# Routing by rounds of the eight largest, five buffers of expert weights, and the residual inside the sums

## The reference

```python
def expert_choice_ffn(h, w_router, w_gate, w_up, w_down):   # h: [1, 256, 1024]
    cap = EC_CAPACITY * S // N_EXPERTS                       # 32 tokens an expert, 16 experts
    aff = jax.nn.softmax(jnp.einsum('bsd,de->bse', h, w_router).astype(jnp.float32), axis=-1)
    g, idx = lax.top_k(aff.transpose(0, 2, 1), cap)          # each expert chooses its 32 tokens
    xe = h[bidx, idx]
    hid = (jax.nn.silu(jnp.einsum('becd,edf->becf', xe, w_gate))   # [1024, 2048] an expert
           * jnp.einsum('becd,edf->becf', xe, w_up))
    ye = jnp.einsum('becf,efd->becd', hid, w_down) * g[..., None].astype(h.dtype)
    return jnp.zeros_like(h).at[bidx, idx].add(ye)
# second_block ends with:
    x = x + expert_choice_ffn(h2, w_router[l], w_gate_e[l], w_up_e[l], w_down_e[l])
    return rms_norm(x, norm_f_g)
```

## Time and profile before

| | us |
|---|---|
| median of three runs | 1643.85 |
| profiled execution | 1641.73 |
| its span | 1639.9 |
| PE busy in the span | 1145.7 (70%) |
| DVE busy | 450.7 (27%) |
| ACT busy | 340.4 (21%) |
| chain that ended last: DMA | 51% |
| chain that ended last: PE | 35% |

### The profile page before, as it was taken

The page is one execution under the profiler, slowest core; times in us unless marked ns, Lnnn a source line. Parts: engine busy times, 40 slices in busy tenths (PEclk is TensorE's granted clock), DMA queues, the critical chain, the costliest instruction groups (busy, mean ns, idle before and its releaser), DMA issues.

```text
span 1639.9 us, 17750 instructions
## 1 busy us (share of the span) xinstructions
PE 1145.7 (70%) x7368; PEld 637.8 (39%) x7372; DVE 450.7 (27%) x742; ACT 340.4 (21%) x548; POOL 153.2 (9%) x119
## 2 busy tenths in 40 slices
PE   3997799996999867575656656566565556565654
PEld 1964798985998867331111111111111111111111
DVE  2457555555696764710000000000000000000001
ACT  3335444443445453100000000000000000000001
POOL 0110000003775300200000000000000000000000
PEclk8999899998999978787777877876888887778787
DMA  9877456553454311569999999999999999999996
GB/s 365 267 298 253 127 173 186 182 196 102 137 155 129 103 52 66 242 285 430 428 429 429 428 428 428 428 428 428 429 428 428 428 429 428 428 428 428 428 428 270
DMA packets 100410, 516.09 MB, mean 315 GB/s; under 512 B 7839, under 2 KB 64650, under 8 KB 72714
## 3 DMA queue, kind: packets, MB, share of 16 engines
q1 hardware_dynamic: 95328, 508.58, 77.2%
q10 hardware_dynamic: 4106, 4.63, 0.9%
q0 software_dynamic: 928, 2.20, 0.5%
HBM read 514.19 MB, written 1.07 MB: 314 GB/s over the span
## 4 chain that ended last, share of the span: by engine, by line
DMA 51%; PE 35%; DVE 9%; ACT 2%; issue 1%; POOL 0%; ACTq 0%; SPq 0%; POOLq 0%; DVEq 0%
DMA ring<-in_w_down_e 26%; DMA ring<-in_w_up_e 24%; PE PS L459 8%; PE PS L460 8%; PE PS L461 8%; PE PS L826 3%; PE PS L843 3%; DVE arena L1102 2%; PE PS L453 2%; DMA ring<-in_w_ada 1%; PE PS L514 1%; DVE arena L1098 1%; PE PS L805 1%; ACT hT L1425 1%; PE PS L593 1%
## 5 line engine op out<-in xcount | busy, mean ns | idle before, releaser
L826 PE MATMUL PS<-ring,arena 128*32 128x512 f32 x2048 | 332.2, 782 | 229.2 <-DMA ring<-in_w_up_e 122.8
L826 PEld LDWEIGHTS PS<-ring,arena 128*32 128x32 f32 x2048 | 63.6, 127 | 490.9 <-DMA ring<-in_w_up_e 207.7
L843 PE MATMUL PS<-ring,arena 128*32 128x512 f32 x1024 | 177.2, 827 | 107.8 <-DMA ring<-in_w_down_e 100.8
L1351 DVE TENSOR_TENSOR arena<-arena,PS 128x512 f32<-128x512 f32 x16 | 11.0, 688 | 865.1 <-PE PS L826 865.1
L459 PE MATMUL PS<-hR,wR 128*128 128x256 f32 x680 | 198.8, 292 | 25.3 <-DVE wR L352 16.0
L344 ACT ACTIVATE wR<-ring 128x1024 fp32r<-128x1024 f32 (+2 forms) x150 | 150.3, 1051 | 226.2 <-PE PS L461 226.1
L460 PE MATMUL PS<-hR,wR 128*128 128x256 f32 x680 | 196.8, 289 | 0.0
L461 PE MATMUL PS<-hR,wR 128*128 128x256 f32 x680 | 196.5, 289 | 0.0
L352 DVE TENSOR_TENSOR wR<-ring,wR 128x1024 fp32r<-128x1024 f32 x106 | 124.9, 1222 | 104.9 <-ACT wR L344 104.9
L459 PEld LDWEIGHTS PS<-hR,wR 128*128 128x128 f32 x680 | 135.2, 199 | 28.0 <-issue 22.4
L460 PEld LDWEIGHTS PS<-hR,wR 128*128 128x128 f32 x680 | 135.2, 199 | 0.1
(11 more groups left out here) (248 smaller groups left out, 1171.1 us busy)
## 6 DMA issues: line engine op xcount, KB each, us to landing
ring<-in_w_gate_e SPq DMA_DIRECT2D x64, 2048.0 KB, 25.9
ring<-in_w_up_e SPq DMA_DIRECT2D x64, 2048.0 KB, 27.3
ring<-in_w_down_e SPq DMA_DIRECT2D x64, 2048.0 KB, 25.9
ring<-in_w SPq DMA_DIRECT2D x32, 1024.0 KB, 5.5
ring<-in_w_in SPq DMA_DIRECT2D x31, 1024.0 KB, 5.4
ring<-in_w_ada SPq DMA_DIRECT2D x24, 1024.0 KB, 7.8
ring<-in_w_out SPq DMA_DIRECT2D x8, 1024.0 KB, 7.3
arena<-bias_scratch POOLq DMA_DIRECT2D x16, 128.0 KB, 6.4
```

The costliest lines, as they stand in the source:

```text
L826: mm = nc.tensor.matmul(PS[32 * j:32 * j + 32, r // 8, :], xe[:, r % 8, :], ring[:, r % RING, 512 * j:512 * (j + 1)], start=(r % 8 == 0), ...
L843: mm = nc.tensor.matmul(PS[32 * q:32 * q + 32, 3, :], hidT[:, chunk % 4, chunk // 4, :], w[:, a, 512 * half:512 * (half + 1)], start=(r == ...
```

## The change

1. **Routing.** `aff` is turned once, to experts by tokens (16 x 256). Four rounds of "the eight largest" and "replace these by -1" mark the 32 largest; a running sum numbers them; two transposes give the ranks by token. `sel` holds a one-hot of the rank for four experts first (`GROUP`), for the other twelve later. The logits are made tokens by experts directly. The matrix of comparisons, POOL's ties, `spread`, `count` and `selTg` are gone.
2. **Gather by groups.** 32 matmuls of 128 moving columns for four experts; the next group's gather stands inside the last expert of a group. `gather_lo` is made by POOL, by halves.
3. **Buffers.** The experts' weights go to five buffers of four slots (`expert_ring`), two of them in `arena`, over what the mixer no longer needs. The first five units are asked for at four points of time; each refill is two loads of 2 MB, each after its half is used (`pairs_used`).
4. **Loops.** The experts' code is written out 16 times on every engine; there is no hardware loop.
5. **Scatter's matrix** is made for each expert: DVE weights `sel` by `aff`, PE turns it (2 transposes), ACT copies it.
6. **Residual.** Four matmuls with the identity put `xres` into the four banks ahead (L787 of the new kernel), so the add at the end is gone; the root's table is asked for ahead, ACT squares and DVE scales out of PSUM, and four half tiles are stored.

The core of the diff:

```diff
-PER_EXPERT = 24
-UNIT = 2
-UNITS = RING // UNIT
+UNIT = 4 * SLOT
+BUFFERS = 5
+FILL = (3, 4, 0, 1, 2)
+UNITS_EACH = 6
+GROUP = 4
...
+        def first_of(u):
+            return 16 * (u // BUFFERS + 1)
+        def halved(u):
+            return u % UNITS_EACH >= 4 or u >= BUFFERS
+        def second_of(u):
+            return 16 * sum(halved(v) for v in range(u % BUFFERS, u + 1, BUFFERS))
...
-            sp.wait_ge(slots_used, PRELUDE)
-            with sp.Fori(0, EXPERTS) as e:
-                for u in range(PER_EXPERT // UNIT):
-                    sp.wait_ge(slots_used, e * PER_EXPERT + used(G_EXPERTS + UNIT * u + UNIT - 1 - RING))
-                    rows = (wg_rows, wu_rows, wd_rows)[u // 4]
...
+            for u in range(EXPERTS * UNITS_EACH):
+                e, kind, b = u // UNITS_EACH, u % UNITS_EACH, u % BUFFERS
+                if u == 0:
+                    sp.wait_ge(normed, 2 * TBRANCH + 2)
+                if u == 1:
+                    sp.wait_ge(mixed, 2)
+                if u == 2:
+                    split_done(sp, PRELUDE - 1)
+                if u == 3:
+                    sp.wait_ge(slots_used, PRELUDE)
+                if u >= BUFFERS:
+                    sp.wait_ge(pairs_used, 2 * (u - BUFFERS) + (1 if halved(u) else 2))
...
-            with pe.Fori(0, EXPERTS) as e:
-                pe.wait_ge(xe_ready, e + 1)
...
+            def gather(group):
+                pe.wait_ge(gather_split, 2)
...
+                for k in range(KD):
+                    o = PS[:, 2 + k // 4, (k % 4) * P:(k % 4 + 1) * P]
+                    for n, (part, t) in enumerate([(gather_hi, 0), (gather_lo, 0), (gather_hi, 1), (gather_lo, 1)]):
+                        mm = nc.tensor.matmul(o, part[:, t, k::KD], sel[t][:, GROUP * group:GROUP * (group + 1), :]
+                                              .rearrange("p e c -> p (e c)"), start=(n == 0), stop=(n == 3))
...
+            gather(0)
+            for e in range(EXPERTS):
...
+                if e % GROUP == GROUP - 1 and e + 1 < EXPERTS:
+                    gather(e // GROUP + 1)
+                    pe.wait_ge(xe_out, 2 * (e // GROUP + 2))
...
+            for n in range(4):
+                rows = PS[0:EXPERTS, 1, 0:S] if n == 0 else left[:, (n + 1) % 2, :]
+                V.max(best8[:, n, :], rows).then_inc(best_set, 1)
+                dve.wait_ge(best_set, n + 1)
+                V.match_replace(left[:, n % 2, :], best8[:, n, :], rows, -1.0).then_inc(left_set, 1)
+                dve.wait_ge(left_set, n + 1)
+            V.tensor_scalar(taken, left[:, 1, :], 0.0, None, ALU.is_lt).then_inc(taken_set, 1)
+            dve.wait_ge(taken_set, 1)
+            V.tensor_tensor_scan(left[:, 0, :], taken, taken, 0.0, ALU.add, ALU.max).then_inc(taken_set, 1)
+            dve.wait_ge(taken_set, 2)
+            V.tensor_tensor(taken, taken, left[:, 0, :], ALU.mult).then_inc(rank_set, 1)
...
+            for t in range(NT):
+                pool.wait_ge(gather_rounded, t + 1)
+                G.tensor_tensor(gather_lo[:, t, :], work[:, t, :], gather_hi[:, t, :], ALU.subtract)\
+                    .then_inc(gather_split, 1)
```

More of the change, by code:

```diff
@@ L242, in build_program @@
         mixin = ybuf
[L244 to L250, removed]
@@ L450, in _ @@
+            for t in range(NT):
+                for half in range(2):
+                    c = slice(512 * half, 512 * (half + 1))
+                    sp.wait_ge(final_set, 2 * t + half + 1)
+                    sp.dma_start(out[0, t * P:(t + 1) * P, c], work[:, t, c]).then_inc(out_stored, 16)
+            sp.wait_ge(out_stored, 16 * 2 * NT)
         @block.tensor
@@ L766, in count @@
[L766 to L803, removed]
-                for n, (part, t) in enumerate([(gather_hi, 0), (gather_lo, 0), (gather_hi, 1), (gather_lo, 1)]):
-                    mm = nc.tensor.matmul(PS[:, k % 4, :], part[:, t, k::KD], sel[:, t, :],
-                                          start=(n == 0), stop=(n == 3))
-                mm.then_inc(gathered, 1)
@@ L809, in _ @@
-            pe.wait_ge(selT_set, 8)
-            pe.wait_ge(rankc_set, 1)
-            for bank in range(4, 8):
-                mm = nc.tensor.matmul(PS[:, bank, :], zeros16[:, :], beats[:, 0, 0:2, :].rearrange("p e t -> p (e t)"),
-                                      start=True, stop=False, skip_group_check=True)
-            mm.then_inc(scattered, 1)
-            pe.wait_ge(xe_out, KD)
-            def unit_arrived(e, r):
-                pe.wait_ge(expert_loaded[r // UNIT % UNITS], e * 32 + 16 * (r // RING + 1))
@@ L820, in _ @@
-            with pe.Fori(0, EXPERTS) as e:
-                pe.wait_ge(xe_ready, e + 1)
-                for r in range(16):
-                    if r % UNIT == 0:
-                        unit_arrived(e, r)
-                    for j in range(4):
-                        mm = nc.tensor.matmul(PS[32 * j:32 * j + 32, r // 8, :], xe[:, r % 8, :],
-                                              ring[:, r % RING, 512 * j:512 * (j + 1)], start=(r % 8 == 0),
-                                              stop=(r % 8 == 7), tile_position=(0, 32 * j))
-                    mm.then_inc(slots_used, 1)
+            for t in range(NT):
+                mm = turn(PS[0:EXPERTS, 1, t * P:(t + 1) * P], aff[:, t, :])
@@ new lines, in _ @@
+            mm.then_inc(aff_rows, 1)
+            for t in range(NT):
+                for half in range(2):
+                    mm = nc.tensor.matmul(PS[:, 4 + 2 * t + half, :], ident, xres[:, t, 512 * half:512 * (half + 1)],
+                                          start=True, stop=False, skip_group_check=True)
+            mm.then_inc(seeded, 1)
+            pe.wait_ge(rank_set, 1)
+            for t in range(NT):
+                mm = turn(PS[:, 0, 32 + t * EXPERTS:32 + (t + 1) * EXPERTS], taken[:, t * P:(t + 1) * P], EXPERTS)
@@ new lines, in gather_out @@
+            def gather_out(group):
+                for part in range(2):
+                    dve.wait_ge(gathered, 2 * group + part + 1)
+                    ks = slice(4 * part, 4 * part + 4)
+                    V.tensor_tensor(xeT[:, group % 2, ks, :], PS[:, 2 + part, :].rearrange("p (k n) -> p k n", k=4),
+                                    gain_rows[:, ks].unsqueeze(2).to_broadcast([P, 4, GROUP * CAP]), ALU.mult)\
+                        .then_inc(xe_out, 1)
+            dve.wait_ge(rank_cols, 1)
@@ L1621, in _ @@
             expect(ACT.Exp)
+            for t in range(NT):
+                N.activation(gather_hi[:, t, :], work[:, t, :], ACT.Copy).then_inc(gather_rounded, 1)
             act.wait_ge(negmax16, 1)
             for t in range(NT):
-                last = N.activation(aff[:, t, :], PS[:, 1, t * EXPERTS:(t + 1) * EXPERTS], ACT.Exp,
+                last = N.activation(aff[:, t, :], PS[:, 0, t * EXPERTS:(t + 1) * EXPERTS], ACT.Exp,
                                     bias=aff_s[:, t:t + 1], accum_out=aff_s[:, 2 + t:3 + t])
@@ L1635, in _ @@
[L1635 to L1641 removed]
+            act.wait_ge(exp16, 1)
+            expect(ACT.Silu)
```

298 lines of the change are left out of this document (147 added, 151 removed).

## The result

The changed kernel took 1597.36 us, median of 4 runs (1595.94 to 1599.91), beside 1643.47 for the kernel before (4 runs): ratio 0.9721, 95% interval 0.9701 to 0.9741. The forecast of 1625 was 28 us too high, and 1597 lies outside its range of 1605 to 1640. It lies between the forecast and rival 1 (1591), much nearer to the rival.

A forecast was written before the change was run, and what follows sets the result against it. The weights' DMA stream at 428 GB/s, after a routing stage with idle DMA, bounds the kernel. -31.1 - 19.6 - 3.7 + 35.5 = -18.9 from 1641.73 gives 1622.8, or 1625 from the median 1643.85; range 1605 to 1640.

The forecast's parts named there:

- rival 1: Weights' stream: instruction fetches cost it next to nothing, +1.5 us; 1591 us in all; chance 0.10.
- Term 4: Weights' stream: 27 fetches of TensorE's written-out program at 1.36 us, all on one DMA engine; +35.5 us.
- Term 1: Routing stage: the stream starts earlier, first expert at 677.5 instead of 708.64; -31.1 us.
- rival 3: Routing's rounds of maxima: 4 us each, first expert at 690, 1638 us in all; chance 0.07.
- Term 2: Weights' stream: 10 loads ahead of it instead of 6, so less is left, without a hole; -19.6 us.
- Term 3: End, from the scatter's start: add and table load leave the path, 8.7 us instead of 12.4; -3.7 us.
- rival 2: Weights' stream: a fetch costs more than 2.0 us of one engine, so slower; 1653 us at 2.4; chance 0.05.

The follow-up runs named there:

- experiment 1: Kernel before, with only TensorE's loop over the experts written out 16 times: 1649.77 us, ratio 1.0039.
- experiment 2: Changed kernel with 420 one-column matmuls, result unread, behind each of the first 15 experts: 1604.53 us, ratio 0.9772.
- experiment 3: Changed kernel with 20 float32 matmuls of 512 columns behind each of the first 15 experts: 1597.91 us, ratio 0.9728.
- experiment 6: Changed kernel with the softmax's last scaling (two 128x16) on ScalarE instead of DVE: 1594.09 us, ratio 0.9694.
- experiment 7: Changed kernel with `gather_hi` laid out so that a matmul's 128 stationary columns are neighbours: 1597.32 us, ratio 0.9722.

## Why the prediction was wrong

**Term 4, instruction fetches, +35.5 forecast, some +5 measured.** This is the step that failed: "I take the same engine each time". The count was right (27 behind the first product, 58 in all), the price of one for the engine that it hits nearly (1.36 seen, 1.5 now), and so was the warning that TensorE's hiding of it doesn't hide it from the stream. Multiplying it by 27 was wrong, since the fetches go to eight engines in turn: the lags lie side by side, and no engine has more than four of them. In the prediction's own sum that is 4 x 1.36, less the one of before, 4.1 in place of 35.5, and 1594. Meanwhile the other engines go on with their share of the nine loads that are queued (46 us from issue to landing), so that the rate stays 428. What is left to see is at the end, where the eight engines without a fetch run dry first and the eight others go on at half the rate. DMA view of the kernel after, 1560 to 1596.1, slices of 0.9 us, and of the kernel before, 1600 to 1640, slices of 1 us:

```profile
GB/s 436 399 436 436 436 436 399 436 418 454 399 472 399 454 418 418 418 436 327 200 218 182 218 91 54 0 0 0 0 0 0 0 0 0 0 54 395 327 381 5
```

```profile
GB/s 459 459 377 426 508 377 426 426 426 459 377 442 475 377 426 492 393 426 426 426 442 393 164 33 0 0 0 0 0 0 0 0 0 0 8 0 279 352 410 8
```

Before falls from 393 to 33 within two slices; after spends seven slices, 6.3 us, between 327 and 54, four of them near 214, half of 428. The prediction had both cases and gave the spread one 0.10, with "nothing in it needs a second engine" as its reason. One fetch in the stream couldn't tell them apart, so 1.4 and 36.9 deserved like chances, and the range a lower end near 1590. Experiments 1 and 2 show the small price, experiment 3 that it is the fetches', and the ends of all streams that eight engines share it. Why eight of the sixteen, and which, no run here shows. The sum had no term for the gain's load (1.2 us).

**Term 1, -31.1 forecast, -29.25 measured.** Right in size, in part by luck: the steps inside were off in both directions. DVE's timeline of the kernel after shows one round:

```profile
664.25 0.42 DVE L1315 MAX8 mgate<-PS 16x8 f32<-16x256 f32 x1 [0.69 <-PE PS L482]
664.71 0.08 DVE L1317 MATCH_VALUE_LOAD top_rows<-mgate,PS 16x8 f32 x1
664.78 0.40 DVE L1317 MATCH_REPLACE8 top_rows<-mgate,PS 16x256 f32<-16x256 f32 x1
...
668.41 0.68 DVE L1321 TENSOR_TENSOR_SCAN top_rows<-top_rows 16x256 f32<-16x256 f32 x1
```

A round took 0.97, four 3.9 (forecast 1.05 and 4.2): taking a pass over 256 numbers as the nearest row was right, and rival 3 is out. POOL's halves took 2.34 each, not 4.83, and were in by 663.52, not last; no run tells why the nearest row was so slow. The gather took 7.93, not 8.5. What was not in the working is that POOL's cover isn't free: experiment 6 measures it at 2.4 us of the first product, and that is most of the 3 us by which the turned `aff` came later than the 661 of the forecast. The residual's matmuls took 5.6, within the 3.4 to 6.8, and ended with the rounds (669.8 and 669.5). The prelude of this execution ended 0.5 later.

**Term 2, -19.6.** Right: 182 loads instead of 186 and no hole. The first refill came 3.30 behind the first product instead of 2.0, since the clock had fallen to 0.53 by the gather's second half and was 0.69 over the first products, where the same stretch of before had 1.00.

**Term 3, -3.7 forecast, -2.5 measured.** The parts of the recorded sum (2.0 + 1.15 + 0.5 + 1.5 + 3.0) make 8.15 and not 8.7, so it should have been -4.3. The order of the end was right. The table load stayed on the path in place of the scatter, which is nearly as long, and the last down product ran at the low clock (3.53 for 1.97). At the higher clock, as in experiment 6, the end is 11.1, and -4.1.

**Slower (rival 2)** needed 2.07 us a fetch and one engine for all of them. With 1.5, and eight engines in turn, it was never near. Part of its mechanism is there, though: a fetch does delay the packet behind it.

## What to carry to other kernels

When each DMA engine is full, price a delay of a single engine by the engine hit most often, not by the sum over all hits, and ask what the trace says on which engine that is; where it says nothing, give both ends of it like chances. Afterwards look at the last microseconds of the stream: how far the rate falls, and for how long, says how many engines are late and by how much. Writing TensorE's loop out costs a weights' stream something, here 5 us in 900, though it is hidden from TensorE. And before an edit takes something off the last chain, look at what ran beside it: the scatter beside the table load, the exponentials behind the copy and the matmuls ahead of `aff` each gave a gain back.

## What the runs showed of the hardware

- A fetch of TensorE's instructions is a packet of 16 KB on q8 and took 1.07 us; the 16 KB weights packet behind it took 1.07 to 1.16 instead of 0.61. Successive fetches lay on eight of the sixteen DMA engines in turn, as far as the packets' times tell, and each cost a full stream of weights 0.18 to 0.20 us (experiments 1 and 2).
- Two scalings of 128x16 in SBUF on DVE: 0.37 us with POOL idle, 3.06 beside POOL's subtraction of 128x1024, until that one ended. On ScalarE they took 0.51 beside it. Not every DVE operation is held: in experiment 6 the first `MAX8` started at 661.98, beside POOL's subtraction (659.12 to 663.77), and took its usual 0.42, and the reciprocal of 128x2 in SBUF took 0.17 at 660.53.
- Float32r matmuls of 128 columns on stationary tiles with a stride of 32 bytes came every 0.24 us at clock 1.00 and 0.53. With the stride gone from every second one, a pair took 0.35 us instead of 0.48 at clock 0.98, and 0.43 at 0.50 (experiment 7).
- ScalarE's copy of 128x1024 took 1.0 us reading in order and 2.0 reading in steps of 32 bytes.
- `MAX8` over 16x256 took 0.42 us, the replacement 0.08 + 0.40, and the running sum 0.68.
